# The latent queries' rotated rows turned into the heads by VectorE instead of TensorE, in a two-block transformer kernel

## The reference

```python
proj = rms_norm(x, g_mix) @ w_in
c_q, c_kv, k_rope, dq, dk, dv = split(proj)
q = (rms_norm(c_q, g_q_lat) @ w_uq).reshape(b, s, 8, 128 + 64)
q_nope, q_rope = q[..., :128], apply_rope(q[..., 128:], cos_r, sin_r)
kv = (rms_norm(c_kv, g_kv_lat) @ w_ukv).reshape(b, s, 8, 128 + 128)
k_nope, v = kv[..., :128], kv[..., 128:]
k_rope = apply_rope(k_rope, cos_r, sin_r)
s = q_nope @ k_nope.T + q_rope @ k_rope.T      # per head
out_mla = softmax(s * 192 ** -0.5) @ v
dq, dk = apply_rope(dq, cos_d, sin_d), apply_rope(dk, cos_d, sin_d)
```

## Time and profile before

| | |
|---|---|
| median of 3 runs | 2400.67 us |
| lowest, highest | 2400.21, 2401.22 us |
| the profiled execution's own time | 2402.68 us |
| its span in the profile | 2400.9 us |
| PE busy | 2386.1 us (99%) |
| DVE busy | 1731.7 us (72%) |
| ACT busy | 1135.2 us (47%) |
| granted TensorE clock over the span | 0.999 |

### The profile page before, as it was taken

One profiled execution on the slowest core, in us unless ns is written; L12 is line 12 of the kernel. 1 busy time (PEld: TensorE's weight loads), 2 busy tenths in 40 slices (PEclk: granted clock), 3 DMA queues, 4 the chain that ended last, 5 costly groups with the idle time before them and its releaser, 6 DMA issues.

```text
span 2400.9 us, 31558 instructions
## 1 busy us (share of the span) xinstructions
PE 2386.1 (99%) x10840; PEld 1987.7 (83%) x10840; DVE 1731.7 (72%) x2356; ACT 1135.2 (47%) x1526; POOL 10.4 (0%) x23
## 2 busy tenths in 40 slices
PE   8999999999999999999999999999999999999999
PEld 7988888888888888888888888888888888888887
DVE  7778777877567756678897977777656765667875
ACT  7554545544444434445554445454444443444553
POOL 0000000000000000000000000000000000000000
PEclk9999999999999999999999999999999999999999
DMA  8645545555555665655556564565656565555654
GB/s 310 217 172 176 167 167 170 190 200 197 195 193 185 201 193 183 203 184 186 183 193 201 177 222 158 193 201 184 203 191 197 179 207 196 188 198 175 209 187 165
DMA packets 126283, 461.97 MB, mean 192 GB/s; under 512 B 14032, under 2 KB 14416, under 8 KB 125408
## 3 DMA queue, kind: packets, MB, share of 16 engines
q1 hardware_dynamic: 123360, 446.22, 55.9%
q0 software_dynamic: 2384, 13.68, 1.7%
q10 hardware_dynamic: 432, 0.59, 0.1%
HBM read 458.35 MB, written 2.10 MB: 192 GB/s over the span
## 4 chain that ended last, share of the span: by engine, by line
PE 94%; DVE 5%; ACT 0%; DMA 0%; issue 0%; ACTq 0%; DVEq 0%
PE acc L460 89%; DVE w_lo L1298 2%; PE acc L655 1%; DVE heads L1433 1%; PE acc L718 1%; PE acc L465 1%; PE po L701 1%; PE po L693 1%; PE pt L540 0%; PE pt L672 0%; DMA raw<-stream 0%; DVE tmp_c L1433 0%; PE acc L501 0%; PE acc L639 0%; DVE tmp_c L1947 0%; DVE tmp_a L1422 0%
## 5 line engine op out<-in xcount | busy, mean ns | idle before, releaser
L1298 DVE TENSOR_TENSOR w_lo<-raw,w_hi 128x1024 fp32r<-128x1024 f32 x844 | 1023.5, 1224 | 559.3 <-ACT w_hi L868 546.2
L868 ACT ACTIVATE w_hi<-raw 128x1024 fp32r<-128x1024 f32 x843 | 890.3, 1060 | 1054.8 <-PE acc L460 951.1
L460 PE MATMUL acc<-w_hi,norm_hi 128*128 128x512 f32 (+1 forms) x2232 | 869.1, 390 | 0.0
L460 PE MATMUL acc<-w_hi,norm_lo 128*128 128x512 f32 (+1 forms) x2232 | 865.6, 388 | 0.0
L460 PE MATMUL acc<-w_lo,norm_hi 128*128 128x512 f32 (+1 forms) x2232 | 594.3, 388 | 0.2
L460 PEld LDWEIGHTS acc<-w_lo,norm_hi 128*128 128x128 f32 x2232 | 417.5, 188 | 87.4 <-DVE w_lo L1298 1.8
L460 PEld LDWEIGHTS acc<-w_hi,norm_hi 128*128 128x128 f32 x2232 | 419.1, 188 | 85.1
L460 PEld LDWEIGHTS acc<-w_hi,norm_lo 128*128 128x128 f32 x2232 | 419.1, 188 | 85.1
L460 PE MATMUL acc<-w_hi,mix_hi 128*128 128x512 f32 x1088 | 426.1, 392 | 3.6 <-ACT w_hi L1111 2.5
L460 PE MATMUL acc<-w_hi,mix_lo 128*128 128x512 f32 x1088 | 424.7, 390 | 0.0
L460 PE MATMUL acc<-w_lo,mix_hi 128*128 128x512 f32 x1088 | 291.7, 390 | 0.0
(11 more groups left out here) (219 smaller groups left out, 916.2 us busy)
## 6 DMA issues: line engine op xcount, KB each, us to landing
raw<-stream SPq DMA_DIRECT2D x843, 512.0 KB, 3.9
x<-x_tok POOLq DMA_DIRECT2D x2, 2048.0 KB, 9.3
heads<-x_in POOLq DMA_DIRECT2D x4, 512.0 KB, 7.7
x<-mem_tok POOLq DMA_DIRECT2D x2, 1024.0 KB, 6.7
heads<-rows_in POOLq DMA_DIRECT2D x2, 1024.0 KB, 8.2
heads<-decay_in POOLq DMA_DIRECT2D x4, 512.0 KB, 5.1
heads<-mem_in SPq DMA_DIRECT2D x3, 512.0 KB, 11.0
out<-x SPq DMA_DIRECT2D x3, 512.0 KB, 5.1
```

What stands on the lines that cost most here:

```text
L460: last = pe.matmul(acc[:, slot, c * NB:c * NB + width], a[:, k * T + c * P:k * T + (c + 1) * P], w[:, s, kk * width:(kk + 1) * width], sta ...
L868: act.activation(w_hi[:, (units.fixed - 1) % RING, :], src, ACT.Copy).then_inc(w_hi_ready, 1)
L1298: dve.tensor_tensor(w_lo[:, s, :], src, w_hi[:, s, :].bitcast(F32), ALU.subtract)\
```

## The change

TensorE's eight transposes behind A1 and ScalarE's copy of them are taken out. VectorE turns the rotated rows of the latent queries by `turn_rows(QR, (i,))`, a quarter behind each of its indices 0 to 3, that is behind the `w_lo` of A4, A5, A6 and A7. The scores of heads 0 and 1 stand behind A4 instead of A3, with the maxima and exponentials one index later too, and wait for `rows_turned`. The counts of `rows_turned` that later waits use grow by one.

```diff
-ROTATED = {"diff": (3, 4), "moba": (8,) * 4, "ret": (12,) * 4}
+ROTATED = {"mla": (1,) * 4, "diff": (4, 5), "moba": (9,) * 4, "ret": (13,) * 4}
...
-        N_ROTATED = 4
+        N_ROTATED = 5
...
-            def turn_rotated():
-                turn(of_block(tmp_a), (rope_ready, rotated.add()), split=False, kept=True)
...
-            whole({1: turn_rotated, 3: lambda: (scores(0), scores(1)), 7: lambda: (transposes(0), transposes(1))})
+            whole({4: lambda: (scores(0), scores(1)), 7: lambda: (transposes(0), transposes(1))})
...
-            during(NU, {0: lambda: mem_squares(0), 1: lambda: evicted(QR), 2: lambda: mem_squares(1),
-                        3: lambda: exps_of(0), 7: lambda: copies_of(0)})
+            during(NU, {0: lambda: mem_squares(0), 2: lambda: mem_squares(1),
+                        4: lambda: exps_of(0), 7: lambda: copies_of(0)})
...
             rotate(lat, cos_n, sin_n, ROPE)
-            evicted.add()
             split(1)
...
-            during(NU, {3: lambda: maxima_of(0), 5: lambda: normalise_of(0), 6: rotate_wide, 7: lambda: first_turn(DQ)})
+            during(NU, {**{i: lambda i=i: turn_rows(QR, (i,)) for i in range(4)}, 4: lambda: maxima_of(0),
+                        5: lambda: normalise_of(0), 6: rotate_wide, 7: lambda: first_turn(DQ)})
```

## The result

| | before | changed |
|---|---|---|
| median of 18 runs each | 2400.94 us | 2405.67 us |
| lowest, highest | 2399.49, 2401.90 | 2404.49, 2407.20 |
| span of the profiled execution | 2400.9 | 2405.4 |

The changed kernel takes 4.73 us more: ratio 1.002, 95% interval 1.0014 to 1.0027. That lies within the 0.2% called no change, at its very edge, and inside the range of 2401.1 to 2405.9, but it is 2.4 us more than the forecast of 2403.3 and 1.4 us above the forecast's own range, which ended at 2404.3. The lowest of the 18 runs is above the highest of before, so the sign is sure.

The account below looks back on a forecast made before the run. TensorE was taken to bound the kernel; -0.91 us for its transposes and +3.47 us of new wait gave +2.56 us, so 2400.67 + 2.6 = 2403.3 us. Its own range was 2402.3 to 2404.3, the wide range 2401.1 to 2405.9.

Parts of the forecast that it names:

- What bounds the kernel: 120 to 150 us window: TensorE alone sets the time, busy 30.00 of 30.00 us; a microsecond there is the kernel's.
- What goes from TensorE: Between A1 and the scores: removing TensorE's transposes with the joins around them gains 0.91 us.
- When TensorE would be ready: At the scores of heads 0 and 1: one unit later and 0.91 us earlier, TensorE is ready at 134.42 us.
- When VectorE has turned the rows: On VectorE: fourth quarter ends at 137.84 us, 12.11 us after the second `w_lo` starts, without waiting for a `w_hi`.
- The new wait: Ahead of the scores: TensorE waits 3.47 us for VectorE's turned rows, with 3.1 and 3.9 as ends.
- Behind the wait: From A5 on: all TensorE work shifts, nothing is earned back and no second wait comes.
- The margins at the exponentials and the division: Behind the scores: exponentials keep 0.84 us of margin; the last division keeps 1.4 us ahead of the probabilities' transposes.
- Sum: Whole kernel: -0.91 + 3.47 = +2.56 us, forecast 2403.3 us, 0.11% longer; chance 0.73.
- rival 1: Behind the new wait: TensorE's clock falls to half, adding 2.5 us, +5.1 in all, 2405.8 us; chance 0.12.
- sign of being wrong: In the changed profile: wait under 1 us, matmuls behind it starting 0.43 us apart, or TensorE waiting again before B0.
- rival 2: At the scores: VectorE keeps up, no wait, -0.91 us, 2399.8; chance 0.04, plus 0.06 for a shorter wait.
- Rivals 2 and 3: The third: late exponentials make TensorE wait again at the transposes behind A7, +3.6 us, 2404.2; chance 0.05.

Follow-up runs that it names:

- e7_scores_five: Changed kernel, but with the scores behind A5 and maxima, exponentials and division at index 5: 2401.93 us against 2400.79 before, ratio 1.0001.
- e1_all_first: Changed kernel, but all 16 stream transposes on VectorE stand together behind the `w_lo` of A4: 2399.87 us against 2400.88 before, ratio 0.9995.
- e4_filled: Changed kernel, but TensorE runs 32 added transposes of the identity matrix between A4 and the scores: 2403.33 us against 2400.88 before, ratio 1.0010.
- e6_one_later: Changed kernel, but each quarter one index later, behind A5, A6, A7 and B0: 2407.85 us against 2400.79 before, ratio 1.0028.

## Why the prediction was right and where it was short

- **What bounds the kernel**: right. What TensorE's chain gained or lost in the stretch is what the medians moved by, within 0.4 us, in the changed kernel and all experiments but e7_scores_five (1.1 us off).
- **What goes from TensorE**, -0.91 us: right; e1_all_first, where nothing else is left, gives -0.92.
- **When TensorE would be ready**, 13.60 us from A0: right to the hundredth (e1_all_first).
- **When VectorE has turned the rows**, 12.11 us from the second `w_lo`: 12.09. The sequence in the earlier trace rows, from another place of the trace, held here. VectorE's share of busy time said that there was room, and the room was in the wrong place. From the start of A4's `w_lo` to the moment at which TensorE is ready are 134.12 - 125.44 = 8.68 us. One `w_lo` and all 16 transposes take 8.33 us (e1_all_first, 123.61 to 131.94) and fit; with three more `w_lo` between the quarters they take 12.09 and don't.
- **The new wait**, 3.47 us: 3.56.
- **Behind the wait**: right that no second wait would come and that nothing is earned back. The margins at the exponentials and the division held.
- **Sum**, +2.56 us: short by the clock. This is the step that failed. It left out a cost that rival 1 had named, and gave that rival 0.12. Its own sign of being wrong came as well: the matmuls behind the wait stand twice as far apart, 0.43 us instead of 0.21 for each of the scores (A5's are at full rate again). That the time lies in the range of 2401.1 to 2405.9 is due to the range, which was drawn to take in rival 1, and not to the mechanism that was forecast. The forecast's own range has a slip of 0.1 us at both ends (its terms give 2402.4 to 2404.2), which changes nothing. The trace shows the fall after 3.56 us of waiting, and filling the wait takes it away (e4_filled). The rival's price was too high, 2.5 us by the earlier trace rows against 1.76, since there a whole unit ran slow and here the slow stretch covered some eight score matmuls. With it the sum is -0.91 + 3.56 + 1.76 = +4.41, and with this rival's right price the forecast would have been 2405.1. The section "HAM oscillation — how this bites in real kernels" of the Trainium skill's page "TensorE: Matmul & The Clock Gate" describes such a case, there with waits for a DMA: a wait that leaves the next piece of work slow. The trace agrees: 0.50 is granted from 0.2 us behind the wait's end, over most of the scores.
- **Rivals 2 and 3**: did not come. What rival 2 priced, -0.91 us without any wait, comes when the turning is moved (e1_all_first), not in the kernel as written.

The change gave TensorE's 0.87 us and ScalarE's 1.03 us of work for 16 instructions and 7.18 us of VectorE. The Trainium skill ("VectorE: DVE Perf Modes", section "Rules for kernel authors") advises TensorE for a transpose of 128 x 128 when PSUM will do as its target. By own time the trace agrees, 0.87 + 1.03 against 7.18 us. But where TensorE bounds the kernel and VectorE has idle time in front of the deadline, the longer way is the cheaper one: e1_all_first is 0.92 us shorter in the stretch. What decided here was when the turning stood, not which engine did it.

## What to carry to other kernels

Room on an engine counts only ahead of the deadline: add up the new sequence step by step to the moment at which it is waited for, and if it misses, issue the waited-for work first and let work with units of slack (here three `w_lo`) come behind it. A wait on a TensorE-bound path costs its length, and one of some 2 us or more, as here with 2.30 us, can cost a spell at half clock on top: price both, the second by the matmuls that stand right behind the wait. When splitting work into portions beside a loop, count the loop's own work that comes to stand between the portions: here three `w_lo`, 3.76 of the 12.09 us.

## What the runs showed of the hardware

The clock stayed up with waits of 0.84, 1.05 and about 1.8 us (1.64 in the list of waits), and fell with 2.30, 3.56 and 5.43 us, each seen in one profile. The moment of the fall is not tied to the wait's end: with 5.43 us it was down while TensorE still stood, with 3.56 us it fell 0.2 us and with 2.30 us about 0.7 us into the scores. By the mean clocks the wait of 3.56 us may have brought the fall in each of 18 runs, since none lists 1.000, while with 2.30 us three of eleven runs had none. What decides between them in one execution, and where the border lies, stays open.

At the head of the kernel before, the granted clock is reported as 1.00 while the distance of matmul starts is 0.43 us, so there the distances are to be believed. In the changed kernel's scores the two agree.

```profile
12.00:14.00 2.00, 2.00 (x6) 1.51 (x6) 1.81 (x4) 2.00 (x4) 0.00 (x0) 1.00 1.05 399
```

A second wait of TensorE for VectorE comes and goes from one execution to the next, without any part of this change. In the changed kernel it lies near 1169 us, ahead of eight transposes, and ends with a multiplication by VectorE that writes their input; the list of waits there reads

```profile
PE pt L540 <- DVE heads L1567: 1.2, 1, 1.2
```

Before, this wait was 0.8 us in the profile, in e6_one_later and e7_scores_five 0.8 and 0.7, and in the other six it was not there. From the transposes of the probabilities to the end, the profiles without it took 2252.8 to 2252.9 us, those with it 2253.8 to 2254.3. So about 0.9 to 1.5 us of the difference between single executions goes with this wait; what brings it was not followed. The profiled executions of both kernels have it, and both are above their medians, by 2.0 us before and 1.5 us in the changed kernel, so it hardly touches the difference between them.
